# Expert search of a two-block layer: search by half heads, comparisons of two rounds on ScalarE, and where a prefix of expert keys is multiplied

## The reference, cut to what matters

```
q = (xb @ w_q).reshape(128, 8, 2, 128)                  # token, head, half, column
s = einsum('thpd,hpnd->thpn', q, sub_keys)              # 128 scores for each half of a head
s_top, i_top = top_k(s, 16)                             # for each half
cand = s_top[:, :, 0, :, None] + s_top[:, :, 1, None, :]    # 16 x 16 pairs
cand_idx = i_top[:, :, 0, :, None] * 128 + i_top[:, :, 1, None, :]
best, pos = top_k(cand.reshape(.., 256), 16)
expert = take_along_axis(cand_idx.reshape(.., 256), pos)
g = softmax(best)
act = gelu(xb . u[expert])
y = sum over (h, k) of (g * act) * v[expert]
```

## Time and profile before

| | us |
|---|---|
| median of three runs | 1432.37 |
| profiled execution | 1430.41 |
| its span | 1428.7 |
| TensorE busy in the span | 1402.6 (98%) |
| VectorE busy | 992.6 (69%) |
| ScalarE busy | 738.5 (52%) |
| GpSimd busy | 183.2 (13%) |
| mean granted TensorE clock | 0.999 of full speed |

### The profile page before, as it was taken

One profiled execution on the slowest core, in us unless ns is written; L12 is line 12 of the kernel. 1 busy time (PEld: TensorE's weight loads), 2 busy tenths in 40 slices (PEclk: granted clock), 3 DMA queues, 4 the chain that ended last, 5 costly groups with the idle time before them and its releaser, 6 DMA issues.

```text
span 1428.7 us, 22032 instructions
## 1 busy us (share of the span) xinstructions
PE 1402.6 (98%) x7854; PEld 1210.0 (85%) x7854; DVE 992.6 (69%) x1748; ACT 738.5 (52%) x1118; POOL 183.2 (13%) x165
## 2 busy tenths in 40 slices
PE   9999999998999999999999999999999999999998
PEld 9888887797788888888888888888889899888886
DVE  6688389899766666666666666666678564665665
ACT  5655311378555555555555555555555734465433
POOL 0072134699000000000000000000000100000000
PEclk9999999999999999999999999999999999999999
DMA  6553530310555555555555555555544432333532
GB/s 212 178 186 109 198 126 31 131 47 16 185 189 189 189 189 191 190 190 186 188 187 190 190 191 190 185 191 185 177 177 170 155 130 107 135 131 147 204 150 103
DMA packets 57510, 229.14 MB, mean 160 GB/s; under 512 B 6752, under 2 KB 9072, under 8 KB 48752
## 3 DMA queue, kind: packets, MB, share of 16 engines
q1 hardware_dynamic: 56992, 228.19, 46.6%
q10 hardware_dynamic: 464, 0.20, 0.1%
HBM read 226.27 MB, written 2.10 MB: 160 GB/s over the span
## 4 chain that ended last, share of the span: by engine, by line
PE 88%; DVE 7%; ACT 2%; issue 1%; POOL 1%; DMA 1%; DVEq 0%; POOLq 0%; ACTq 0%
PE ps L2343 23%; PE ps L2116 17%; PE ps L2332 13%; PE ps L2082 8%; PE ps L2330 8%; PE ps L2318 4%; PE ps L2038 3%; PE ps L2328 2%; PE ps L2157 2%; PE ps L2295 1%; DVE lo L1402 1%; PE ps L1996 1%; DMA raw<-in_v_t 1%; PE ps L2460 1%; PE ps L2453 1%
## 5 line engine op out<-in xcount | busy, mean ns | idle before, releaser
L1641 DVE TENSOR_TENSOR lo<-raw,hi 128x1024 fp32r<-128x1024 f32 x234 | 286.0, 1222 | 61.7 <-ACT hi L1049 61.7
L2332 PE MATMUL ps<-x,hi 128*128 128x512 f32 x826 | 296.8, 398 | 0.0
L1049 ACT ACTIVATE hi<-raw 128x1024 fp32r<-128x1024 f32 x234 | 245.9, 1051 | 0.0
L2330 PE MATMUL ps<-x,lo 128*128 128x256 f32 x944 | 245.6, 281 | 0.0
L2116 PE MATMUL ps<-hi,x 128*128 128x512 f32 x704 | 224.8, 393 | 0.6 <-DVE lo L1402 0.4
L1402 DVE TENSOR_TENSOR lo<-raw,hi 128x2048 fp32r<-128x2048 f32 x60 | 140.1, 2336 | 72.8 <-ACT hi L894 72.8
L2330 PEld LDWEIGHTS ps<-x,lo 128*128 128x128 f32 x944 | 178.5, 189 | 9.2
L2332 PEld LDWEIGHTS ps<-x,hi 128*128 128x128 f32 x826 | 155.2, 188 | 33.1
L1104 ACT ACTIVATE oi<-ps 128x256 f32<-128x256 f32 x118 | 45.4, 385 | 229.6 <-PE ps L2332 228.5
L2116 PEld LDWEIGHTS ps<-hi,x 128*128 128x128 f32 x704 | 132.2, 188 | 28.9 <-issue 1.5
L2343 PE MATMUL ps<-hi,wh 128*128 128x512 f32 x484 | 150.4, 392 | 1.3 <-DVE wl L1655 1.1
(11 more groups left out here) (402 smaller groups left out, 2271.4 us busy)
## 6 DMA issues: line engine op xcount, KB each, us to landing
raw<-in_v_t SPq DMA_DIRECT2D x128, 512.0 KB, 3.5
raw<-in_u_t SPq DMA_DIRECT2D x126, 512.0 KB, 3.5
raw<-in_pieces SPq DMA_DIRECT2D x61, 1024.0 KB, 4.8
ring<-in_peer_w_q SPq DMA_DIRECT2D x4, 2048.0 KB, 8.1
big<-in_up SPq DMA_DIRECT2D x4, 2048.0 KB, 8.6
ring<-in_w_mem_kv SPq DMA_DIRECT2D x1, 2048.0 KB, 7.7
resid<-in_x SPq DMA_DIRECT2D x2, 512.0 KB, 4.4
raw<-in_pieces SPq DMA_DIRECT2D x2, 512.0 KB, 7.7
```

What stands on the lines that cost most here:

```text
L1049: act.activation(hi[:, which, par], raw[:, which, par], ACT.Copy).then_inc(hi_done[which], 1)
L1641: dve.tensor_tensor(lo[:, which, par], raw[:, which, par], hi[:, which, par].bitcast(F32), ALU.subtract).then_inc(lo_done[which], 1)
L2330: pe.matmul(first, u_lo[:, par, c], xh[:, c], start=False, stop=False)
L2332: ins = pe.matmul(both, u_hi[:, par, c], x2[:, :, c], start=False, stop=(c == KC - 1))
```

## The change

Rounds 0 and 1 are computed on TensorE by half heads: 8 portions of 16 records, each into a bank of its own (three in rotation), one step of `memory` behind each, and then two score products of 128 columns. Rounds 2 and 3 go by head. VectorE waits for each half of head 0 in rounds 0 and 1 by itself; head 1 of those rounds, and both heads of rounds 2 and 3, are searched a head at a time. The places get two buffers, and in rounds 0 and 1 VectorE leaves the comparison out; ScalarE makes it as relu(1 - |place - slot|), with 16 Abs instructions (one slot each, 64 elements, result written with a stride of 16) and one Relu over 1024, from `compare_places`, which stands at four points between copies. GpSimd waits on ScalarE for those rounds. `CHUNKS_BEFORE_PICKS` goes from 32 to 20, `CHUNKS_BEFORE_BUILD` from 44 to 32 (48 chunks among the half groups), `BLOCKS_BEFORE_PICKS` from 4 to 2. Two semaphores are renamed and get more meanings.

```
-BY_HEAD = 2
-CHUNKS_BEFORE_PICKS = 32
-CHUNKS_BEFORE_BUILD = 44
-BLOCKS_BEFORE_PICKS = 4
+BY_HALF = 2
+ACT_ROUNDS = 2
+CHUNKS_BEFORE_PICKS = 20
+CHUNKS_BEFORE_BUILD = 32
+BLOCKS_BEFORE_PICKS = 2
...
+        half_bank = {f"wq{r}{h}{b}": (4 * r + 2 * h + k) % 3 for r in range(BY_HALF) for h in range(2) for k, b in enumerate(("", "b"))}
...
-        place = takeP(2, NT * 2, TOP)
+        places_of = takeP(2, 2, NT * 2, TOP)
...
+        score_groups = [(r, n, slice(a, a + 1)) for r in range(BY_HALF) for a in range(4) for n in range(NT)]
+        score_groups += [(r, n, slice(2 * h, 2 * h + 2)) for r in range(BY_HALF, ROUNDS) for h in range(2) for n in range(NT)]
+        def scores_until(r, h, a=1):
+            return 8 * r + 4 * h + 2 * a + 2 if r < BY_HALF else 8 * BY_HALF + 4 * (r - BY_HALF) + 2 * h + 2
...  GpSimd, in each round
-                    pool.wait_ge(matched, 2 * r + k + 1)
+                    if r < ACT_ROUNDS:
+                        pool.wait_ge(logf_then_act_matched, 1 + 2 * r + k + 1)
+                    else:
+                        pool.wait_ge(matched, 2 * (r - ACT_ROUNDS) + k + 1)
...  ScalarE
+            def out_half(r, h, a):
+                g = f"wq{r}{h}" + ("b" if a else "")
+                act.wait_ge(group_done, group_no[g] + 1)
+                act.activation(qT[:, 4 * r + 2 * h + a], ps[:, gbank(g), 0:T], ACT.Copy).then_inc(group_out, 1)
+            def compare_places(r, k):
+                kept = pick[:, r % 2, (1, 0)[k]]
+                act.wait_ge(fgate_then_places_done, 1 + r + 1)
+                for i in range(TOP):
+                    act.activation(kept[:, :, :, i], places_of[:, r % 2, (1, 0)[k]], ACT.Abs, scale=-1.0, bias=iota[:, i:i + 1]).then_inc(act_step, 1)
+                steps[0] += TOP
+                act.wait_ge(act_step, steps[0])
+                flat_kept = kept.rearrange("p c k i -> p (c k i)")
+                act.activation(flat_kept, flat_kept, ACT.Relu, scale=-1.0, bias=1.0).then_inc(logf_then_act_matched, 1)
+            for r in range(BY_HALF):
+                for h in range(2):
+                    for a in range(2):
+                        out_half(r, h, a)
+                        out_scores(8 * r + 4 * h + 2 * a, 8 * r + 4 * h + 2 * a + 2)
+            compare_places(0, 0)
             out_query(2, 0)
+            out_scores(16, 18)
+            compare_places(0, 1)
             out_query(2, 1)
-            out_scores(8, 10)
+            out_scores(18, 20)
+            compare_places(1, 0)
             out_query(3, 0)
+            out_scores(20, 22)
+            compare_places(1, 1)
             out_query(3, 1)
-            out_scores(10, 12)
+            out_scores(22, 24)
...  VectorE, in each round
+                for h in range(2):
+                    if r < BY_HALF and h == 0:
+                        for a in range(2):
+                            dve.wait_ge(sub_out, scores_until(r, h, a))
+                            search(halves[a::4])
+                    else:
                         dve.wait_ge(sub_out, scores_until(r, h))
                         search(halves[2 * h:2 * h + 2] + halves[4 + 2 * h:4 + 2 * h + 2])
-                        search_pairs((h,))
-                else:
-                    dve.wait_ge(sub_out, scores_until(r))
-                    search(halves)
-                    search_pairs((0, 1))
+                    search_pairs((h,))
...
+                if r >= 2:
+                    dve.wait_ge(logf_then_act_matched, 1 + 2 * (r - 2) + 2)
...
+                if r < ACT_ROUNDS:
+                    dve.tensor_tensor(place[:, 1], p1, p4, ALU.subtract).then_inc(fgate_then_places_done, 1)
+                    continue
...  TensorE
+            def half_features(r, h, a):
+                need(f"wq{r}")
+                g, f0 = f"wq{r}{h}" + ("b" if a else ""), (2 * h + a) * P
+                bank_free(g)
+                for c in range(KC):
+                    ins = pe.matmul(ps[:, gbank(g), 0:T], tile_view(f"wq{r}")[:, c, f0:f0 + P], actT[:, c], start=(c == 0), stop=(c == KC - 1))
+                ins.then_inc(group_done, 1)
+                return g
+            for r in range(BY_HALF):
+                for h in range(2):
+                    for a in range(2):
+                        k = 4 * r + 2 * h + a
+                        g = half_features(r, h, a)
+                        memory(19 + k, 20 + k)
+                        if k == 0:
+                            pe.wait_ge(cols_then_mem_loaded, 96)
+                        key_scores(2 * k, 2 * k + 2, g)
+            features("wq2", actT, (0,))
             memory(27, 29)
+            key_scores(16, 18, "wq20")
+            features("wq2", actT, (1,))
             memory(29, 31)
+            key_scores(18, 20, "wq21")
+            features("wq3", actT, (0,))
+            key_scores(20, 22, "wq30")
+            features("wq3", actT, (1,))
+            memory(31, 32)
+            key_scores(22, 24, "wq31")
+            memory(32, MEM_STEPS)
```

More of the change, by code:

```diff
@@ L238, in build @@
         group_out = sem("group_out")
-        fgate_done = sem("fgate_done")
-        logf_done = sem("logf_done")
+        fgate_then_places_done = sem("fgate_then_places_done")
+        logf_then_act_matched = sem("logf_then_act_matched")
         gate_mm = sem("gate_mm")
@@ L347, in build @@
                    "hgate0", "hgate1", "ggate0", "ggate1",
-                   "mk0", "wq00", "wq01", "wq10", "wq11", "wq20", "wq21", "wq30", "wq31", "mk1", "mv0", "mv1"]
+                   "mk0", "wq00", "wq00b", "wq01", "wq01b", "wq10", "wq10b", "wq11", "wq11b", "wq20", "wq21", "wq30", "wq31", "mk1", "mv0", "mv1"]
         group_no = {g: i for i, g in enumerate(groups1)}
+        half_bank = {f"wq{r}{h}{b}": (4 * r + 2 * h + k) % 3 for r in range(BY_HALF) for h in range(2) for k, b in enumerate(("", "b"))}
         mem_bank = {"mk0": 2, "mk1": 3, "mv0": 2, "mv1": 3}
@@ L355, in gbank @@
                 return mem_bank[g]
+            if g in half_bank:
+                return half_bank[g]
             return int(g[3]) if g[:2] == "wq" else group_no[g] % 4
         def tile_used(name):
-            return group_done, group_no[name + "1"] + 1
+            return group_done, group_no[name + ("1b" if name in ("wq0", "wq1") else "1")] + 1
         takeP = arena(big[:], NKEY * T)
@@ L932, in _ @@
             split_2nd_after("glow")
-            act.wait_ge(fgate_done, 1)
-            act.activation(feat(gF[:, 0:4]), feat(gF[:, 0:4]), ACT.Ln).then_inc(logf_done, 1)
+            act.wait_ge(fgate_then_places_done, 1)
+            act.activation(feat(gF[:, 0:4]), feat(gF[:, 0:4]), ACT.Ln).then_inc(logf_then_act_matched, 1)
             act.wait_ge(gate_mm, 1)
@@ L1439, in _ @@
             wait_marked()
-            dve.tensor_scalar(kF[:, 0:4], gF[:, 0:4], -1.0, 1.0, ALU.mult, ALU.add).then_inc(fgate_done, 1)
+            dve.tensor_scalar(kF[:, 0:4], gF[:, 0:4], -1.0, 1.0, ALU.mult, ALU.add).then_inc(fgate_then_places_done, 1)
             piece_split_lo("gqk1", "glow", "hi0", "hi1")
@@ L1446, in _ @@
             piece_split_lo("gv0")
-            dve.wait_ge(logf_done, 1)
+            dve.wait_ge(logf_then_act_matched, 1)
             for f in range(NF):
@@ L1573, in search_pairs @@
                         mark(dve.max_index(pos[:, n, h, 8:16], best[:, n, h, 8:16], crest[:, k]))
-                if r < BY_HEAD:
-                    for h in range(2):
+                for h in range(2):
[4 more added lines that the diff above has]
+                    else:
                         dve.wait_ge(sub_out, scores_until(r, h))
                         search(halves[2 * h:2 * h + 2] + halves[4 + 2 * h:4 + 2 * h + 2])
-                        search_pairs((h,))
-                else:
-                    dve.wait_ge(sub_out, scores_until(r))
-                    search(halves)
-                    search_pairs((0, 1))
+                    search_pairs((h,))
                 mark(dve.tensor_copy(sidxf[:, r], sidx[:, r]))
@@ L1596, in _ @@
                 link(dve.tensor_copy(posf, posi))
+                place = places_of[:, r % 2]
+                if r >= 2:
+                    dve.wait_ge(logf_then_act_matched, 1 + 2 * (r - 2) + 2)
                 p1, p4, p16 = (posf[:, k].rearrange("p n (h k) -> p (n h) k", h=2) for k in range(3))
@@ L2168, in _ @@
             pe.wait_ge(softplus_done, 1)
-            pe.wait_ge(fgate_done, 1)
+            pe.wait_ge(fgate_then_places_done, 1)
             scores(0, qF, kF)
```

31 lines of the change are left out of this document (2 added, 29 removed).

## The result

| | before | after |
|---|---|---|
| median us (five runs each) | 1432.37 | 1438.70 |
| lowest to highest | 1430.00 to 1432.56 | 1437.70 to 1439.89 |
| profiled execution, its span | 1430.41, 1428.7 | 1439.42, 1437.7 |

The ratio of the times is 1.0048 [1.0037, 1.0059]. I had forecast 1432.2 (1429.9 to 1434.4); the kernel is 6.3 us slower and lies outside the range.

What follows compares the result with a forecast made beforehand. Prediction: TensorE (88% of the span) and VectorE run side by side and meet at the picks. Picks -2.2, gelu stop +1.13 and six build groups +0.93 sum to -0.15 us: median 1432.2, range 1429.9 to 1434.4.

Steps and rivals of the forecast that it cites:

- VectorE's sum up to the picks: VectorE's work before the picks: the terms sum to +2.2 us, picks at 269.5 instead of 271.68.
- five terms: Comparisons removed +4.56, round 2's wait removed +1.18, round 0's head 1 later -0.97, smaller batches -0.41 and -2.14 us.
- a rival in which GpSimd itself ends last: Before the picks: late masks make GpSimd the bound, 1.9 us behind the last comparison, 1434.1 us; chance 8%.
- TensorE idle 1.9 us before the picks: TensorE is at the picks at 267.6 and waits 1.9 us for VectorE, which ends last.
- half portion: TensorE in rounds 0 and 1: half a head's products, laid-bare query copy and scores take 4.64 us.
- half start: Round 0: VectorE searches head 0's first half 4.2 us sooner, but waits some 3 us for head 1 anyway.
- fourth rival: Round 0: the half start does nothing, showing as 3 us of idle before head 1; counted inside the forecast.
- first rival: Rounds 0 and 1: ScalarE's comparisons outlast the gap between copies, deciding from 7.7 us each; 1440.2 at 9.0; chance 10%.
- second rival: GpSimd becomes the bound before the picks, its masks ending 1.9 us behind the last comparison: 1434.1 us; chance 8%.
- stop for the gelu: Early in the build: chunk 32 waits for the third gelu behind ScalarE's evacuation of half group 0, +1.13 us once.
- six groups more with chunks: The build: six groups more carry two chunks each at 0.155 us a group, +0.93 us.
- third rival: Faster: laid-bare copies and the gelu stop do not show, 1430.2, or 1429.2 with small batches free; chance 17%.

Runs made afterwards that it cites:

- nofold: The changed kernel with GpSimd's multiplication and folding of the masks left out in rounds 0 and 1: 1431.01 us, ratio 0.9998.
- beforelate: The kernel before with one wait more, holding GpSimd's first mask until VectorE's candidate sum of head 1 in round 1: 1438.07 us, ratio 1.005.
- filler: The changed kernel with 24 products that nobody reads on TensorE ahead of its wait for the picks: 1435.51 us, ratio 1.003.
- headact: The kernel before with rounds 2 and 3 by head and ScalarE's comparisons in rounds 0 and 1; whole heads there, old chunk plan: 1432.57 us, ratio 1.0007.
- plan44: The changed kernel with the chunk plan of before (32, 44 and 4 blocks): 1434.31 us, ratio 1.0019.
- early: The changed kernel with whole heads in rounds 0 and 1, earlier ScalarE comparisons, masks held for searches, gelus 2 and 3 first, 28 and 40 chunks: 1431.46 us.
- before20: The kernel before with only the chunk plan changed (20, 32 and 2 blocks): 1436.06 us, ratio 1.0028.
- acts0: The changed kernel with all comparisons back on VectorE: 1439.85 us, ratio 1.0057.

## Why the prediction was wrong

**The step that failed is VectorE's sum up to the picks**, "4.56 + 1.18 - 0.97 - 0.41 - 2.14 = +2.2". Its five terms are about right: nofold, which has them all, puts the picks at 96.7 (forecast 96.9). What is missing is a sixth term, of -4.56 us: I moved GpSimd's masks in time and charged nothing for it, except as a rival in which GpSimd itself ends last. The rows show it apart from the sum. In after the sums and the comparisons of round 2 are too long by 5.2 in all (2.14, 0.19, 0.63 and 0.09 at `L1586`, 2.16 at `L1638`), in nofold the sums by 0.5 (one takes 0.86, one 0.51); the difference of 4.7 is what the picks differ by (101.40 and 96.71). That the sixth term equals the first is chance.

The signs were in what I had read. The earlier trace rows have GpSimd's mask at 3.27 us, beside the second comparison of 262.65; others of the same line take 2.35 (229.34). I read this as a price of GpSimd's. It was the wait for VectorE's second comparison, and a wait that goes one way had to raise the question of the other, which the 3.25 at 265.04 answers. The Trainium skill says it outright, in the page "SBUF — State Buffer", section "SBUF: two separate sides": VectorE and GpSimd share a pair of ports under an exclusive lock, held for a whole instruction, which VectorE wants when it has two SBUF inputs or runs in a two-port mode. The trace agrees (0.44 to 2.58 for two inputs). The conversions are held too (0.40 to 1.34 and 0.26 to 0.66, beforelate); whether they run in a two-port mode no run here shows. Had I used it, the rival "masks fall on sums and comparisons" would have stood in the prediction at +5 us.

**A second term was missing, +2.4: the clock behind the wait.** I had TensorE idle 1.9 us before the picks and charged no clock. With 6.14 it was granted 0.91 over the next stretch, and 0.63 + 1.77 were lost. filler shows that it is the idleness. The 1.9 itself was never run; the nearest is nofold, with 1.52 and a clock of 1.00, so no run speaks against charging nothing for the forecast wait. The term follows from the first one, which made the wait long.

Point by point for the rest:
- A half portion takes 4.64 us (183.15 to 187.79), as worked out (3.455 + 0.64 + 0.54).
- VectorE's wait before head 1 of round 0 is 3.38 (forecast "some 3"), with head 1 at 19.24 after the first product (forecast 19.3). The half start gains nothing, as the fourth rival said, and costs about the 1.38 that the sum has for it (headact against plan44).
- ScalarE's comparison takes 5.06 (forecast 4.9), with 1.6 to spare; the first rival's condition isn't met. GpSimd is idle 6.16 before its last mask; the second rival isn't either.
- TensorE reaches the first key at 86.05 (forecast 85.96). The stop for the gelu is 1.21 (1.13), the six groups more with chunks cost 1.15 (0.93).
- The forecast of faster (third rival) held in no part.

In the profiled executions the change costs 6.8 us (9.0 less the 2.25 ahead of it). The forecast of -0.15, the two missing terms (4.56 + 2.40) and the small errors above (0.08 + 0.22 - 0.37) add up to 6.74. That they meet is no proof by itself, since the 4.56 and the 2.40 are measured less forecast; nofold, filler and the rows above are.

## What to carry to other kernels

When a change moves work of GpSimd, or of VectorE beside it, lay both timelines next to each other: a mutual stop doesn't show as idle time but as an instruction that is longer than its siblings of the same line and shape. Use GpSimd where VectorE does MAX8, FIND_INDEX8 and MATCH_REPLACE8, and count up to a full GpSimd instruction for every two-operand or converting VectorE instruction that it may meet. And size the work that TensorE does ahead of a wait by when the awaited thing comes: too much hides a gain (early), too little is paid twice, once idle and once in clock (before20).

## What the runs showed of the hardware

- VectorE and GpSimd stop each other for the rest of the instruction that is running: 0.23 us became 2.26, and GpSimd's folds 4.26 for 2.5 (beforelate). VectorE's conversions of one input are stopped as well (0.40 to 1.34). Its MAX8, FIND_INDEX8 and MATCH_REPLACE8 aren't: in early they lie beside the mask of 208.98 at their usual lengths.
- TensorE's granted clock, by the idle time right before the picks: 0.20, 0.58, 0.85, 1.15 and 1.52 us, 1.00 in 260 to 300; 4.08, 4.69, 6.14, 6.17, 7.40 and 7.41 us, 0.91; 7.94 us, 0.87. Price in transposes and twelve chunks: 2.4 us in after, 1.6 (before20) to 2.9 (acts0) in the seven. No run has an idle time between 1.52 and 4.08.
- A clock of 0.91 in 40 to 60 us, in 8 of the 15 profiled executions, with old and new code, goes with a first query product 1.0 to 2.9 us later. The spread of the times of before is as large, and the mean clock parts it: of 87 executions of before beside the experiments, the 47 with 0.998 took 1431.6 to 1433.0 and the 38 with 0.999 took 1429.3 to 1431.0 (two with 1.000: 1430.9 and 1431.3). What makes the clock fall there wasn't tested.
